# Output projection moved behind the attention units, in three rounded passes, with its weight streamed in sixteen pieces

## The reference

```python
h = rms_norm(x, norm_mix[1])
q, k, v = attn_project(h, w_qkv, q_gain, k_gain)      # 1024 x 3072
o = softmax(q k^T / 8 + relative bias, own and earlier chunks) v
x = x + o @ w_o                                       # w_o is 1024 x 1024: the output projection
h = rms_norm(x, norm_ffn[1])
group, experts, gates = route(h)                      # top group, then top 2 of its 8 experts
x = x + sum over the 2 experts e of gate * ((silu(h @ w_gate[e]) * (h @ w_up[e])) @ w_down[e])
```

## Time and profile before

| | us |
|---|---|
| median of 3 timed runs | 1343.85 |
| the three runs | 1343.29, 1343.85, 1345.46 |
| span of the profiled execution | 1340.0 |

### The profile page before, as it was taken

How to read it: one execution, slowest core, us unless ns; L and a number is a source line. 1 busy time by engine, 2 the same in 40 slices (tenths; PEclk the granted TensorE clock), 3 DMA queues, 4 the chain that set the end, 5 groups by cost and what they waited for, 6 DMA issues and landing times.

```text
span 1340.0 us, 19743 instructions
## 1 busy us (share of the span) xinstructions
PE 1291.8 (96%) x7448; PEld 638.2 (48%) x7448; DVE 574.1 (43%) x1062; ACT 304.7 (23%) x650; POOL 127.9 (10%) x205
## 2 busy tenths in 40 slices
PE   8899999999999999999999999899999999999998
PEld 6643344333343334788777544443444334343333
DVE  4543334433333433864419543543334334343433
ACT  4211111111111113443436432211111111111111
POOL 2010000000000000232233210000000000000000
PEclk9989999999999999999999999899999999999999
DMA  9989999999999999222058512999999999999996
GB/s 360 380 334 420 424 428 426 427 429 427 428 427 427 428 425 402 69 93 97 34 174 273 181 33 78 380 344 420 426 427 426 427 428 428 427 428 427 426 426 255
DMA packets 53569, 459.65 MB, mean 343 GB/s; under 512 B 8141, under 2 KB 9421, under 8 KB 28170
## 3 DMA queue, kind: packets, MB, share of 16 engines
q1 hardware_dynamic: 41246, 426.48, 76.5%
q0 software_dynamic: 9616, 23.95, 5.5%
q10 hardware_dynamic: 2652, 8.45, 1.7%
HBM read 455.44 MB, written 11.26 MB: 348 GB/s over the span
## 4 chain that ended last, share of the span: by engine, by line
PE 91%; issue 3%; DVE 3%; ACT 2%; DMA 1%; POOL 0%; SPq 0%; DVEq 0%; ACTq 0%; POOLq 0%
PE ps L2014 34%; PE ps L2045 11%; PE ps L2023 9%; PE ps L2024 8%; PE ps L2443 4%; PE ps L1843 3%; PE ps L1845 3%; PE ps L1844 3%; PE ps L2006 2%; PE ps L2377 1%; PE ps L2393 1%; PE ps L1916 1%; PE ps L2032 1%; PE ps L2353 1%; PE ps L1864 1%
## 5 line engine op out<-in xcount | busy, mean ns | idle before, releaser
L1592 DVE TENSOR_TENSOR x<-x,ps 128x1024 f32<-128x1024 f32 (+1 forms) x150 | 177.7, 1216 | 220.9 <-PE ps L2045 219.8
L1606 DVE SCALAR_TENSOR_TENSOR nat<-nat,slot_gate,ps 64x256 f32<-64x256 f32 x128 | 86.1, 672 | 196.3 <-ACT nat L1093 164.7
L2014 PE MATMUL ps<-pair,xT 128*64 128x512 f32 x352 | 163.8, 616 | 6.1 <-issue 6.1
L2014 PE MATMUL ps<-ring,xT 128*64 128x512 f32 x352 | 160.9, 606 | 8.0 <-issue 6.4
L2015 PE MATMUL ps<-pair,xT 128*64 128x512 f32 x352 | 164.0, 616 | 0.0
L2045 PE MATMUL ps<-y_parts,hot 64*128 64x512 f32 (+1 forms) x1200 | 161.3, 403 | 0.0
L2015 PE MATMUL ps<-ring,xT 128*64 128x512 f32 x352 | 161.1, 607 | 0.0
L2014 PE MATMUL ps<-third_pair,xT 128*64 128x512 f32 x320 | 143.6, 596 | 6.9 <-issue 6.9
L1093 ACT ACTIVATE nat<-ps 64x512 f32<-64x512 f32 x62 | 36.8, 594 | 485.5 <-PE ps L2015 485.5
L2024 PE MATMUL ps<-qk,hidT 128*64 128x512 f32 x320 | 144.9, 595 | 0.0
L2023 PE MATMUL ps<-qk,hidT 128*64 128x512 f32 x320 | 144.8, 595 | 0.0
(11 more groups left out here) (261 smaller groups left out, 1780.3 us busy)
## 6 DMA issues: line engine op xcount, KB each, us to landing
qk<-in_moe_w_down SPq DMA_DIRECT2D x40, 2048.0 KB, 28.5
ring<-in_moe_w_down SPq DMA_DIRECT2D x22, 2048.0 KB
ring<-in_moe_w_gate SPq DMA_DIRECT2D x20, 2048.0 KB, 23.7
ring<-in_moe_w_up SPq DMA_DIRECT2D x20, 2048.0 KB
third_pair<-in_moe_w_gate SPq DMA_DIRECT2D x20, 2048.0 KB, 22.7
third_pair<-in_moe_w_up SPq DMA_DIRECT2D x20, 2048.0 KB
pair<-in_moe_w_gate SPq DMA_DIRECT2D x18, 2048.0 KB
pair<-in_moe_w_up SPq DMA_DIRECT2D x18, 2048.0 KB, 29.7
```

What stands on the lines that cost most here:

```text
L1592: return V.tensor_tensor(x[0:n, i, :], x[0:n, i, :], ps[0:n, bank:bank + 2, :].rearrange("p b c -> p (b c)"), ALU.add)
L1606: last = V.scalar_tensor_tensor(out=out[u * BLK:(u + 1) * BLK, :].rearrange("s (k p) -> s k p", k=n), in0=act_rows[:, u * n:(u + 1) * n, : ...
L2014: mm(ps[BLK:P, GU_BANK, :], rows, gate[:, at], start=(k == 0), stop=(k == KT - 1))
```

## The change

The projection leaves the units and stands behind them, but for 12 products. Both factors are split into a rounded part and the rest (`oT_hi`, `oT_lo`; `wo_part(c, 1)`, `wo_part(c, 0)`), in the rounded type fp32r, and a product is three matmuls (hi hi, lo hi, hi lo), as in the QKV projection. ACT rounds (`oT_rounded`, `wo_rounded`), DVE subtracts (`oT_rest`, `wo_rest`). The 16 pieces of `w_o` (k = 0 to 7 in two halves of 512 columns, 256 KB each) lie in places that are free at that time: `ring` 0, `nat`, `gain`, `xT`. `pair` is free, so gate 1 and up 1 are loaded during the attention. ACT now takes both heads' transposes of the short units out of PSUM in one instruction. Squares, scaling and storing of rows 1 to 3 for the router move behind the projection.

```diff
+        WO_EARLY, WO_SPLIT = 33, 28
+        def early_products(t):
+            items = [(k, i) for k in range(WO_QUAD) for i in range(TILES - 1, 0, -1)]
+            return items[2 * (t - WO_EARLY):2 * (t - WO_EARLY) + 2] if t >= WO_EARLY else []
...
+                    sp.wait_ge(s_ps, 2)
+                    load_gate(1, 1, 1)
+                    sp.wait_ge(s_ps, PAIRS)
+                    load_up(1, 1, 1)
                     sp.wait_ge(s_ps, LONG_UNITS)
                     load_down(1, 1, 1)
                     sp.wait_ge(pT_ps, 2 * LONG_UNITS)
-                    load_gate(1, 0, 0)
+                    for c in range(WO_QUAD):
+                        load_wo(c)
                     sp.wait_ge(s_ps, PROMPT_UNITS)
                     load_down(1, 2, 2)
-                    sp.wait_ge(oT_sb, OT_ALL)
+                    sp.wait_ge(o_ps, UNITS)
+                    for c in range(WO_QUAD, KT):
+                        load_wo(c)
+                    load_up(1, 0, 0)
...
-                    sp.wait_ge(att_y, 2 * NT)
-                    load_gate(l, 1, 1)
-                    load_up(l, 1, 1)
...
@@ ACT, in iteration t
+                if group_at(t, OT_GROUP + 4) is not None:
+                    oT_rounded(group_at(t, OT_GROUP + 4))
+                if 0 <= t - WO_SPLIT < WO_QUAD:
+                    wo_rounded(t - WO_SPLIT)
...
@@ DVE, in iteration t
-                for i, hf in halves_before(t):
-                    add_product(i, hf)
-                if 0 <= t - 2 < PROMPT_UNITS:
+                if 0 <= t - 2 < LONG_UNITS:
                     pT_out(t - 2)
+                if group_at(t, OT_GROUP + 5) is not None:
+                    oT_rest(group_at(t, OT_GROUP + 5))
+                if 0 <= t - WO_SPLIT - 1 < WO_QUAD:
+                    wo_rest(t - WO_SPLIT - 1)
...
@@ TensorE
+            def part_product(hf, i, k):
+                c = hf * KT + k
+                pe.wait_ge(split_lo, QKV_QUARTERS + c + 1)
+                return split_product(ps[:, WO_BANKS[hf][i], :], oT_hi[:, k, tok(i)], oT_lo[:, k, tok(i)],
+                                     wo_part(c, 1), wo_part(c, 0), k == 0, k == KT - 1)
...
-                if products_at(t) is not None:
-                    tile_product(*products_at(t))
+                for k, i in early_products(t):
+                    part_product(0, i, k)
+            for k in range(WO_QUAD):
+                part_product(0, 0, k)
+            for k in range(WO_QUAD):
+                last = sample_product(0, k)
+            last.then_inc(quarters_used, 1)
+            for k in range(WO_QUAD, KT):
+                for i in range(TILES - 1, -1, -1):
+                    last = part_product(0, i, k)
+                last = sample_product(0, k)
...
+            pe.wait_ge(std_ready, 3 * NT + TILES - 1)
             transposes(3, TILES - 1)
-            for hf in range(2):
-                sample_product(hf)
             route(1)
```

More of the change, by code:

```diff
@@ L290, in encoder, with wo_part, wo_raw @@
         rw_experts = xT_flat[:, KT * NG:KT * NR].rearrange("p (g n) -> p g n", g=NG)
+        def wo_part(c, part):
+            where, u = WO_PLACES[WO_PLACE[c]]
+            return wo_parts[where][:, u, part, :]
+        def wo_raw(c):
+            where, u = WO_PLACES[WO_PLACE[c]]
+            flat = (ring[:, 0, :], nat[:, :], gain[:, :], xT_flat)[where]
+            return flat[:, u * 1024:u * 1024 + 512]
         early_rows = third_pair[:, 1, :]
@@ L305, in encoder @@
                  for u in range(2)]
+        pT_both = [a4[:, 2 * D + u * 1024:2 * D + (u + 1) * 1024].rearrange("p (h n) -> p h n", h=2) for u in range(2)]
         BIASES_RING, BIASES = 3, 5
@@ L1292, in _ @@
             for t in range(UNITS + 4):
[L1293 to L1294 removed]
+                if group_at(t, OT_GROUP + 3) is not None:
+                    oT_out(group_at(t, OT_GROUP + 3))
                 if t < UNITS:
@@ L1300, in _ @@
                     pT_out(t - 2)
-                for i, hf in halves_before(t - 1):
-                    if hf == 1 and i > 0:
-                        early_squares(i)
+                if group_at(t, OT_GROUP + 4) is not None:
+                    oT_rounded(group_at(t, OT_GROUP + 4))
+                if 0 <= t - WO_SPLIT < WO_QUAD:
+                    wo_rounded(t - WO_SPLIT)
                 if t == UNITS:
                     load_sqrt_table()
-                    act.wait_ge(act_own, own[0])
-                    act.activation(std[:, 3, 1:TILES], ssq[:, 3, 1:TILES], ACT.Sqrt, bias=const("eps"),
-                                   scale=1.0 / D).then_inc(std_ready, TILES - 1)
-            oT_out(UNITS - 1)
+            oT_out(GROUPS_OUT)
+            oT_rounded(GROUPS_OUT)
+            for c in range(WO_QUAD, WO_PARTS):
+                wo_rounded(c)
             for i in range(TILES - 1, 0, -1):
-                store_row(1, i)
+                early_squares(i)
+            act.wait_ge(act_own, own[0])
+            act.activation(std[:, 3, 1:TILES], ssq[:, 3, 1:TILES], ACT.Sqrt, bias=const("eps"),
+                           scale=1.0 / D).then_inc(std_ready, TILES - 1)
             first_chunks(1, TILES - 1)
@@ L1324, in _ @@
             store_row(1, NT - 1)
+            for i in range(TILES - 1, 1, -1):
+                store_row(1, i)
             logitsT_out(1, 1)
+            store_row(1, 1)
             route_exps(1)
```

249 lines of the change are left out of this document (161 added, 88 removed).

## The result

The changed kernel takes 1349.76 us (median of 9 runs), the kernel before 1343.85 in the same series. The ratio that the measurement gives is 1.0051, with a 95% interval of 1.0040 to 1.0061 (the two medians alone give 1.0044): slower by half a per cent. Forecast were 1340.3 us, faster, with a range up to 1346.5. The profiled execution spans 1346.8 us, against 1340.0.

A forecast was written before the change was run, and what follows sets the result against it. TensorE was taken to bound the projection, the weight stream the second expert stage. Terms 2.7 + 1.8 - 0.1 - 0.5 - 0.3 = 3.6 us took 1343.85 to 1340.3 us; 8-in-10 range 1336 to 1346.5.

The forecast's parts named there:

- What bounds: Second expert stage bound by its weight stream, only its start can move; TensorE bound from 736.5 to 840.3 us.
- Step 1: Projection: 64 products at 0.689 us instead of 0.91, 44.1 us instead of 58.1, saving 14.0 us.
- step 2: Samples: 32 matmuls of 512 columns one behind another, adding 7.3 us up to the last product.
- Step 3: Attention units without products: lost cover costs nothing, added rounding work on ACT and DVE loses 4 us, bounds 0 to 10.
- Step 4: Last product to logits: fold at +3.7 us, gain 1.8 us; gather waiting for stores put at 0, up to 2.
- Step 5: TensorE's clock in the routing may fall during the first logits: cost 0 to 2 us, taken as 0.5.
- Step 6: Late w_o pieces in the projection: 4 us remain for the way of the DMA; cost 0.3 us, bounds 0 to 3.
- rival A: Clock falls to 1.2 GHz in the short units without products: 8.4 us more, 1348.7 us, slower; chance 0.10.
- Step 7: Preloading gate 1 and up 1 is alone worth nothing; the stream from up 2 to the end stays 467.6 us.
- Rival B: Bias loads fall behind in the attention, adding some 5 us: 1345.3 us, no gain; chance 0.20.
- Rival C: Preload takes 9.8 us out of the weight stream behind the routing: 1330.5 us, far faster; chance 0.03.

The follow-up runs named there:

- the pieces early: Changed kernel without the preload, pieces 4 to 11 of w_o loaded into `pair` during the attention: 1340.86 us, ratio 0.9986 to the kernel before.
- The float32 kernels: Kernel before with all 16 float32 product groups behind the units, nothing rounded there: 1359.1 us; with bias corners blanked two units after their load as well: 1355.62 us.
- the filler: Kernel with early w_o pieces, plus one unread 128x256 float32 matmul in each iteration from t = 24 to 32: 1341.41 us, ratio 0.9990.
- bias loads deeper: Changed kernel with a bias's corner blanked two units after its load was issued, not one: 1347.97 us, ratio 1.0035 to the kernel before.
- the float32 kernel with deeper bias loads: Kernel before with float32 products behind the units and bias corners blanked two units after their load: 1355.62 us, ratio 1.0093.
- own counts: Changed kernel with a semaphore for each of pieces 4 to 7 and 12 to 15: 1347.68 us; with gate 0 loaded behind pieces 12 to 15 too: 1346.82 us.

## Why the prediction was wrong, step by step

**What bounds.** Right. The second stage is as long as its bytes; from up 2 to the end all fourteen kernels take 466.8 to 468.7 us, whatever stands in front. TensorE bound the projection, and saved time on it counted as long as nothing took its place.

**Step 1, products at 0.689 us, and step 2, samples at 7.3.** Right. With the pieces early 54 products and the samples take 44.6 us, by the forecast's prices 44.5.

**Step 3, units without products, 4 us lost.** Undersized: 7.3 to 7.7 were lost, and the reason was another. I put the missing cover at nothing and the rounding at 4. The float32 kernels show the reverse: without any rounding 8.9 us are lost, and 3.5 (85.5 - 82.0) where the clock holds in the prompt units. Of the changed kernel's loss 2.3 us lie in the prompt units (74.71 against 108.73 - 10 x 3.63 = 72.4) and 5.0 in the samples (21.5 - 6.9 = 14.6 against 27.7 - 18.2 = 9.6). Most of the latter is the clock: with the filler, which holds it, that part takes about 11.1 us (19.0, less 6.9 of products and two fillers of some 0.5), 3.5 less, and 2.8 less than in the same kernel without the filler (13.9). What makes up the 2.3 us in the prompt units stays open: with bias loads deeper, or with nothing rounded, or both, the units take 74.5 to 74.7 us.

**Step 4, the tail.** Right in its mechanism: the fold at +3.6 (forecast 3.7), the first logits at +8.2 (8.4), a gain of 2.1 (1.8). The bound of up to 2 us for a gather that waits for the stores, which I valued at 0, cost 1.0.

**Step 5, the clock in the routing,** 0.5: not seen apart; the stretch to up 2 is accounted for without it.

**Step 6, pieces of w_o, 0.3 us with bounds of 0 to 3.** This is the step that failed and turned the sign. In the changed kernel's trace it cost 1.75 + 2.70 us of waiting and 3.0 of half clock; in the two others with these waits the half clock cost 1.4 and 1.6, and the whole 6.7 and 6.4 instead of 7.9. I counted 4 us for the way of the DMA and the transfer of one piece. One piece does take 4.3 us, but the wait is for four: 6.4 us, and 6.7 behind gate 0's bytes. I had the count in the code, and a row that warned of the other: a bias load of 9.6 us behind 2 MB loads. And the upper bound left out what a pause does to the clock, although rival A is about nothing else.

**Step 7, the preload worth nothing.** Right, and dearer than that: it took the place in which the pieces can lie early.

**Rival A** (the clock falls in the short units) did happen, in every kernel with the units as the changed one has them, and stands behind the larger part of step 3's miss. At 8.4 us it was too dear: the clock falls only at about 776, where the prompt units end, and costs about 3. In 765 to 775 of the kernel with early pieces TensorE is busy for 8.3 of 10 us at 1.00, then it falls. The Trainium skill, in "TensorE: Matmul & The Clock Gate", section "Part 4: PE-mode transpose", has transposes not count as activity. By that rule a filler of plain matmuls should hold the clock where transposes don't, and it did; but in the float32 kernel with deeper bias loads it held as well, up to about 784, with no matmul added and fewer pauses. Pauses fit what happens at 776 in all the traces; the fall at 784, with none right ahead of it, they leave open. Whether transposes count is not decided here.

**Rival B** (bias loads fall behind) had the right picture. In the changed kernel's profiled execution a load held POOL for 7.8 us, and five units of lead swallowed it. In the two kernels above with the preload and own counts it came through, with 4 and 2 us. In the medians it is small: without the preload, or with deeper bias loads, the ratio stayed within the interval's width. The Trainium skill, in "DMA: Bandwidth & Descriptors", section "Queues, rings and completion order", has the engines take turns between queues packet by packet; by that rule a small load passes a large one. The 9.6 us of the earlier trace rows disagree, and so does the changed kernel, where the bias load of 256 KB issued at 742.92, beside down 1, took 9.9 us. **Rival C** did not come.

The sum, by what was measured at the last product: 3.3 (units, 7.3 lost instead of 4), 7.9 (pieces and their clock) and 0.3 (a later start) make 11.5, against 848.9 - 837.6 = 11.3.

## What to carry to other kernels

Work between the steps of a latency-bound loop is cover and keeps TensorE's clock; price its removal by a run that removes it alone. A load that is issued when it is needed costs its whole way, here 4.3 us for one piece of 256 KB, 6.4 for four that count together, 6.7 to 7.1 behind other bytes. A pause of TensorE behind it can be paid a second time at half clock: the four waits of 2.6 to 3.2 us in the projection were, the four of 1.3 to 1.8 us were not. A buffer given to a load that nobody waits for is taken from one that is waited for.

## What the runs showed of the hardware

A wait of TensorE of 1.75 us at 804 left the clock at 1.00; one of 2.70 us at 826 was followed by 6.3 us at 0.52, those of 2.64, 2.75 and 3.15 us in three other kernels by 3.6, 3.2 and 2.7 us at half clock. The length of the pause is not all: in the units, where shorter pauses had gone before, one of 1.75 us at 756 was followed by half clock too. The four issues of pieces 4 to 7 took SP 3.12 us, those of 12 to 15 only 1.75. And one store of 512 KB needed 11.1 us beside a 2 MB load; with that load held back the slowest store took 5.1 us.
